# Merged distance-and-maximum operation in two attentions, and two more expert weight slots

## The chip, the cores and the metric

The kernel runs on 1 core of one Trainium2 chip. The metric is the device time of one execution in microseconds (us), the median of several runs. All data are float32. The engines that matter here are TensorE (PE, with its weight loads as PEld), VectorE (DVE), ScalarE (ACT), and SyncE (SP), whose queue issues nearly all DMA transfers.

## What is computed

Two transformer blocks over 256 tokens of width 1024. The first block has two layers; each has a mixer of three attentions (MLA, differential, sliding window), a cross-attention and a dense feed-forward. The second block is one layer with a recurrence, a pooling branch, a grouped attention, and a mixture of 16 experts. The change touches the scores of two of the attentions and the loading of the expert weights.

```python
# differential attention: 4 heads, 2 maps each
s = einsum('bqhmd,bshmd->bmhqs', qi, k2) * scale
s = s - slopes * abs(pos_q - pos_k)
p = softmax(s); a = p[:, 0] - lam * p[:, 1]
# sliding window: 8 heads, a sink per head
s = einsum('bnqkgd,bnskd->bnkgqs', qg, kb) * scale
s = s - slopes * dist; s = where(mask, s, lowest)
m = maximum(max(s), sink); e = exp(s - m)
p = e / (sum(e) + exp(sink - m))
...
# experts (expert choice): 16 experts, 32 tokens each, width 1024
# every expert's gate, up and down matrices are read once
```

## The kernel before

**Weights.** All weight matrices lie in one HBM array, `in_stream`, cut into units of 128 x 2048 float32 (1 MB). SP's queue copies them into SBUF slots in the order in which TensorE uses them. In the two layers there are 8 slots (5 called `ring`, 3 in `arena`), 64 units to a layer (L3417). In the second block the 35 dense units go through the 5 ring slots (`dense_unit`, L3426): unit v is issued when TensorE has finished the unit that held its slot, five units earlier. Each slot has a semaphore that counts its landings.

**Experts.** The last 192 units are the expert weights. They have 21 slots (`EXPERT_SLOTS`), made of the five ring slots and of pieces of `arena`, `par` and `const` that come free as the second block's other work ends. SP issues the first 14 (`EARLY_SLOTS`) as these pieces come free: three after the recurrence (`recurrence_left`), then in five batches (`BRANCHES_LEFT`), with the last dense units between them; then five ring slots as the dense units leave them, then two more. From the 22nd unit on, each waits until TensorE has used the unit that is 21 places before it (`expert_slots_used`, L3457). TensorE starts on the experts when the router has chosen the tokens.

**Attention scores.** Each layer works through 20 items in the order of `HEAD_ITEMS`: 4 MLA heads, 8 differential maps, 8 sliding-window heads. TensorE writes the scores of an item for both blocks of 128 tokens into one PSUM bank (L1034); differential and sliding-window items come in pairs and two banks (`both_tiles`) serve in turn, so that a pair waits until the banks of the pair before are read. VectorE then makes, for each differential or sliding-window item, one 128 x 512 operation that adds the distance times minus slope over scale to the raw scores (L1052), a maximum over each row (L1056), for a sliding-window head one more small operation with the sink (L1060), and the negated maximum (L1062, L1064). ScalarE takes the exponentials with the scale as an argument (L1077); VectorE normalises (L1094 to L1100) and for a second differential map subtracts (L1109); TensorE transposes (L1129); ScalarE copies the transposed tile (L1259) and TensorE multiplies by the values (L1162, L1178), whose result ScalarE copies out (L1250, L1255, L1888). All engines run their queues in program order. Between these steps TensorE runs fill work: three matmuls of the cross-attention's memory projections at each step (`MEMORY_HEADS`). After the last item VectorE forms differences of weights for the output projection (L740).

**Queries and keys.** Five units project them into columns; ScalarE copies each result from PSUM to `qk` (L1874), two 256-column pieces in one 128 x 512 operation: differential queries (j = 0), their keys (1), sliding-window queries (2, 3), their keys (4, 256 columns). Right behind j = 3 the memory rows are transposed (L203, L472) into the same two ScalarE banks (`act_tiles`) and copied with their gain (L490).

Of the kernel before, what the change touches and what calls it, by code (L numbers as in the profile page):

```python
# [20 lines left out]
S = 256  # L21
# [11 lines left out]
EARLY_SLOTS = 14  # L33
EXPERT_SLOTS = TOP_SLOTS + RING_SLOTS + 3
# [11 lines left out]
FAR = 1e30  # L46
LAYER_UNITS = 64
# [8 lines left out]
def columns(*parts):  # L56
# [9 lines left out]
    ("ident", 128), ("inv", 16), ("iota", 32), ("fold", E_N), ("eps", 1), ("ln_eps", 1), ("half_pi", 1),  # L66
# [20 lines left out]
GATE_UNITS = 12  # L87
ROUTER_ROWS = (0, 0, 0, E_N)
# [87 lines left out]
class Weights:  # L176
# [6 lines left out]
    def start(self, base, slots, loaded, free):  # L183

        self.n, self.base = 0, base
# [31 lines left out]
class Program:  # L217
    def __init__(self, nc, ctx, io):
# [8 lines left out]
                   *(f"expert_slot_loaded_{s}" for s in range(EXPERT_SLOTS)),  # L227
# [4 lines left out]
        self.expert_slot_loaded = [self.sem(f"expert_slot_loaded_{s}") for s in range(EXPERT_SLOTS)]  # L232
# [20 lines left out]
        self.expert_slots = (top[7:10] + ends + [top[0], top[1], top[5], top[12], halves, top[11]] + [top[4], top[6], top[10]]  # L253
# [681 lines left out]
SCALE = {"gqa": 64 ** -0.5, "diff": 32 ** -0.5, "swa": 64 ** -0.5, "mla": 96 ** -0.5, "x": 256 ** -0.5}  # L935
# [103 lines left out]
def softmax_max_dve(p, dve, i, item):  # L1039
# [15 lines left out]
    dve.e.wait_ge(p.both_tiles.drained, p.both_tiles.taken["dve"])  # L1055
    dve.e.tensor_reduce(mx, sc, AX, ALU.max).then_inc(dve.step(), 1)  # L1056
    dve.e.wait_ge(dve.steps, dve.n)
    if kind == "swa":
# [3 lines left out]
        dve.e.tensor_scalar(nm, mx, -1.0, None, ALU.mult).then_inc(dve.event("max_found"), 1)  # L1062
    else:
# [788 lines left out]
def layer_act(p, act, l, layer_par, mem_rows):  # L1852
# [17 lines left out]
    for j in range(5):  # L1870
# [3 lines left out]
        act.e.activation(p.qk[:, 2 * j:2 * j + n, :], shaped(bank[:, 0:n * S], n, S), ACT.Copy).then_inc(p.act_tiles.drained, 1)  # L1874
# [384 lines left out]
def second_pe(p, pe, w):  # L2259
    w.start(16 * DEPTH * LAYER_UNITS // SLOTS, p.ring_slots, p.slot_loaded, p.slots_free)  # L2260
# [1414 lines left out]
```

## Time and profile before

| | us |
|---|---|
| median of 3 runs | 1803.08 (1802.34 to 1803.63) |
| the profiled execution | 1804.25 |
| its span in the trace | 1802.5 |
| TensorE busy | 1627.3 (90%) |
| VectorE busy | 784.2 (44%) |
| ScalarE busy | 373.5 (21%) |
| HBM read | 383.65 MB |

The first layer runs to about 475 us, the second to about 935 us, the second block without its experts to about 1358 us, and the experts from there to the end. The page divides the span into 40 slices of 45 us: in the slices up to the 29th TensorE is at 9 tenths or more, and from the 32nd on the DMA engines are at 9 while TensorE falls to 6 or 7. A row of the timeline gives start, duration, engine, line, operation, output and inputs, count, and in square brackets how long the engine was idle before it and what released it.

### The profile page before, as it was taken

How to read it: one execution, taken by the hardware profiler on the slowest of the kernel's cores; microseconds unless marked ns; L12 is line 12 of the kernel's file. 1: busy time of each engine (PE TensorE's matmuls, PEld its weight loads, DVE VectorE, ACT ScalarE, POOL GpSimd, SP SyncE). 2: the span in 40 equal slices, each digit the busy share in tenths (PEclk: the TensorE clock that was granted, in tenths of full speed). 3: DMA queues.
4: the chain of work that ended last, by engine and by line, in shares of the span. 5: the costliest groups of instructions: out<-in, count | busy, mean ns of one | idle time of the engine just before them, and what ended most of it. 6: DMA issues, size and time to landing. Idle time of an engine off the chain costs nothing.

```text
span 1802.5 us, 26083 instructions
## 1 busy us (share of the span) xinstructions
PE 1627.3 (90%) x10862; PEld 1098.7 (61%) x10862; DVE 784.2 (44%) x1514; ACT 373.5 (21%) x953; POOL 2.2 (0%) x6
## 2 busy tenths in 40 slices
PE   8999999999999999999999999999999667667666
PEld 5867878884587787888558778888854101102011
DVE  3596567655539755765655583131421000000001
ACT  4253131110415412211021651111221000000001
POOL 0000000000000000000000000000000000000000
PEclk9999999999999999999999999999999866877766
DMA  9324335435542242543444231111788999999997
GB/s 388 118 71 145 136 118 203 182 146 188 219 145 75 105 167 77 197 187 146 187 164 147 87 116 51 49 59 63 303 323 325 421 421 421 421 421 420 421 420 321
DMA packets 55664, 386.35 MB, mean 214 GB/s; under 512 B 6272, under 2 KB 6784, under 8 KB 10752
## 3 DMA queue, kind: packets, MB, share of 16 engines
q1 hardware_dynamic: 53568, 375.15, 52.8%
q10 hardware_dynamic: 1984, 9.57, 1.4%
q8 instruction: 87, 1.43, 0.3%
q14 instruction: 25, 0.20, 0.0%
HBM read 383.65 MB, written 1.05 MB: 213 GB/s over the span
## 4 chain that ended last, share of the span: by engine, by line
PE 68%; DMA 22%; DVE 6%; ACT 2%; issue 1%; SPq 0%; PEldq 0%; DVEq 0%; PEld 0%; ACTq 0%
PE ps L199 49%; DMA arena<-in_stream 13%; DMA ring<-in_stream 6%; PE ps L2216 3%; DMA const<-in_stream 3%; PE ps L2197 3%; PE ps L1513 2%; PE ps L1034 2%; DVE small L1056 1%; PE ps L203 1%; DVE arena L1052 1%; PE ps L688 1%; PE ps L2357 1%; DVE arena L1100 1%; PE ps L1188 1%
## 5 line engine op out<-in xcount | busy, mean ns | idle before, releaser
L199 PE MATMUL ps<-arena 128*128 128x256 f32 (+4 forms) x2476 | 572.2, 498 | 77.3 <-DMA arena<-in_stream 71.9
L199 PEld LDWEIGHTS ps<-arena 128*128 128x128 f32 (+1 forms) x2476 | 324.2, 169 | 283.0 <-DMA arena<-in_stream 162.1
L199 PE MATMUL ps<-ring,arena 128*128 128x256 f32 (+5 forms) x1186 | 336.6, 526 | 39.3 <-DMA ring<-in_stream 34.4
L199 PE MATMUL ps<-arena,ring 128*128 128x256 f32 (+1 forms) x1228 | 284.2, 378 | 0.0
L199 PEld LDWEIGHTS ps<-ring,arena 128*128 128x128 f32 (+1 forms) x1186 | 177.6, 174 | 172.4 <-issue 76.4
L199 PEld LDWEIGHTS ps<-arena,ring 128*128 128x128 f32 x1228 | 221.1, 191 | 37.2 <-issue 9.9
L2527 PE MATMUL ps<-arena 128*32 128x512 f32 x230 | 153.7, 772 | 0.0
L2734 DVE TENSOR_TENSOR arena<-arena,ps 128x512 f32<-128x512 f32 x8 | 5.5, 687 | 250.5 <-PE ps L2527 250.5
L2749 DVE TENSOR_TENSOR x<-x,ps 128x512 f32<-128x512 f32 (+1 forms) x18 | 11.3, 628 | 139.3 <-PE ps L2629 139.3
L1077 ACT ACTIVATE arena<-arena,small 128x256 f32<-128x256 f32 x112 | 55.7, 498 | 76.0 <-DVE small L1064 76.0
L2527 PE MATMUL ps<-ring,arena 128*32 128x512 f32 x84 | 60.0, 816 | 0.0
L1660 ACT ACTIVATE arena<-arena 128x512 f32<-128x512 f32 x20 | 12.6, 630 | 179.4 <-DVE arena L1716 179.4
L1034 PE MATMUL ps<-arena 64*128 64x256 f32 (+3 forms) x256 | 46.8, 392 | 1.9 <-DVE arena L1052 1.3
L1690 DVE TENSOR_TENSOR arena<-ring,arena 128x1024 f32<-128x1024 f32 x38 | 45.4, 1221 | 2.1
L1056 DVE TENSOR_REDUCE small<-arena 128x2 f32<-128x512 f32 x56 | 38.4, 686 | 1.9
L1034 PEld LDWEIGHTS ps<-arena 64*128 64x128 f32 (+3 forms) x256 | 32.6, 187 | 10.0 <-issue 4.1
L1513 PE MATMUL ps<-arena 128*128 128x256 f32 x128 | 38.1, 379 | 0.0
L2216 PEld LDWEIGHTS ps<-arena 64*64 64x64 f32 x1152 | 34.4, 135 | 3.3 <-issue 3.3
L199 PE MATMUL ps<-par,arena 128*32 128x512 f32 x90 | 26.7, 823 | 10.0 <-DMA const<-in_stream 5.8
L2216 PE MATMUL ps<-arena 64*64 64x32 f32 x1152 | 35.5, 219 | 0.0
L1100 DVE TENSOR_SCALAR arena<-arena,small 128x256 f32<-128x256 f32 x112 | 34.5, 350 | 2.0
L1129 PE MATMUL ps<-const,arena 128*128 128x128 f32 x192 | 29.9, 279 | 4.6 <-ACT arena L1255 4.1
(431 smaller groups left out, 1887.1 us busy)
## 6 DMA issues: line engine op xcount, KB each, us to landing
arena<-in_stream SPq DMA_DIRECT2D x168, 1024.0 KB, 24.9
ring<-in_stream SPq DMA_DIRECT2D x160, 1024.0 KB, 6.4
par<-in_stream SPq DMA_DIRECT2D x9, 1024.0 KB, 26.7
const<-in_stream SPq DMA_DIRECT2D x9, 1024.0 KB, 27.0
par<-in_layer_par ACTq DMA_DIRECT2D x3, 1664.0 KB, 8.2
par<-in_stream SPq DMA_DIRECT2D x9, 512.0 KB, 24.2
const<-in_stream SPq DMA_DIRECT2D x9, 512.0 KB, 24.6
arena<-in_mem ACTq DMA_DIRECT2D x2, 1024.0 KB, 10.7
```

Of the source, the lines that this page charges most:

```text
L199: ins = self.pe.e.matmul(out, lhsT, rhs, start=start, stop=stop)
L203: return self._tell(self.pe.e.transpose(out, in_, identity))
L1034: ins = pe.e.matmul(bank[:, b * S:(b + 1) * S], a, k, start=j == 0, stop=j == len(parts) - 1)
L1056: dve.e.tensor_reduce(mx, sc, AX, ALU.max).then_inc(dve.step(), 1)
L1077: ins = act.e.activation(p.pr[i % 4][:, b, :], p.sc[i % 4][:, b, :], ACT.Exp, bias=nm[:, b:b + 1], scale=SCALE[kind], accum_out=sums[:, b: ...
L1100: ins = dve.e.tensor_scalar(pr[:, b, :], pr[:, b, :], sums[:, b:b + 1], None, ALU.mult)
L1129: ins = pe.e.transpose(bank[:, o:o + P], src[:, b, kb * P:(kb + 1) * P], p.c("ident"))
L1513: ins = (pe.e.matmul if end and last else w.mm)(out, left[:, k, :], right[:, k, :], start=k == 0, stop=end)
L1690: dve.e.tensor_tensor(t[n], a, b, ALU.subtract).then_inc(dve.event("weight_sums"), 1)
L2197: ins = pe.e.matmul(bank[r, o, :], a, b, start=j == 0, stop=j == len(ts) - 1)
L2216: ins = pe.e.matmul(bank[r, o, :].rearrange("p (g s) -> p g s", s=1 << n), left[r, o, :], rhs)
L2527: ins = (pe.e.matmul if e == GE - 1 else w.mm)(bank[r, :], src[:, k, r], slot_columns(u, e * 512, 512), start=k == 0, stop=k == KC - 1)
```

## The change

Three things are changed.

1. In differential and sliding-window items, the distance operation and the row maximum become one operation for each token block of 128 rows (`tensor_tensor_reduce` on 128 x 256): (scores minus distance) times slope, with the running maximum started from a very low number, or from the head's sink. The scale and the slope's inverse are moved into the query rows, so that the exponential's scale becomes 1.0.
2. For that, ScalarE's copies of the query projections (j = 0, 2, 3) are each made in two 128 x 256 operations with a factor for each row (`query_gain`, six new columns of the constants).
3. The SBUF that the compiler sets aside for DMA descriptors is cut to 512 bytes a partition, and two more expert slots (`spare`, 16 KB a partition) take its place. They are the first two of the slots' order, 23 in all, and are filled in the second block behind dense units 18 and 20. Their landings are counted on the semaphores of two layer slots, so the waits get a base for each slot.

```diff
-EARLY_SLOTS = 14
-EXPERT_SLOTS = TOP_SLOTS + RING_SLOTS + 3
+EARLY_SLOTS = 16
+SPARE_SLOTS = 2
+EXPERT_SLOTS = SPARE_SLOTS + TOP_SLOTS + RING_SLOTS + 3
...
+SPARE_AFTER = (18, 20)
...
-        self.pe.e.wait_ge(self.loaded[s], self.base + 16 * len(slot_parts(self.slots[s])) * (r + 1))
+        self.pe.e.wait_ge(self.loaded[s], self.bases[s] + 16 * len(slot_parts(self.slots[s])) * (r + 1))
...
+        spare = self.sb("spare", SPARE_SLOTS * UNIT)
+        spares = [spare[:, j * UNIT:(j + 1) * UNIT] for j in range(SPARE_SLOTS)]
+        self.expert_slots = (spares + top[7:10] + ends + [top[0], top[1], top[5], top[12], halves, top[11]] + [top[4], top[6], top[10]]
...
-SCALE = {"gqa": 64 ** -0.5, "diff": 32 ** -0.5, "swa": 64 ** -0.5, "mla": 96 ** -0.5, "x": 256 ** -0.5}
+DIFF_SCALE, SWA_SCALE = 32 ** -0.5, 64 ** -0.5
+SCALE = {"gqa": 64 ** -0.5, "diff": 1.0, "swa": 1.0, "mla": 96 ** -0.5, "x": 256 ** -0.5}
...
-        dve.e.scalar_tensor_tensor(sc, dist, -slope / scale, bank, ALU.mult, ALU.add).then_inc(p.both_tiles.drained, 1)
+        lowest = LOWEST if kind == "diff" else p.lp("sinks")[:, h:h + 1]
+        for b in range(NB):
+            ins = dve.e.tensor_tensor_reduce(sc[:, b, :], bank[:, b, :], dist[:, b, :], slope, lowest, ALU.subtract, ALU.max,
+                                             accum_out=mx[:, b:b + 1])
+            if b == NB - 1:
+                ins.then_inc(p.both_tiles.drained, 1)
+            else:
+                ins.then_inc(dve.step(), 1)
+        dve.e.wait_ge(dve.steps, dve.n)
+        dve.e.wait_ge(p.both_tiles.drained, p.both_tiles.taken["dve"])
+        dve.e.tensor_scalar(nm, mx, -1.0, None, ALU.mult).then_inc(dve.event("max_found"), 1)
...
-        dve.e.tensor_scalar(mx, mx, scale, p.lp("sinks")[:, h:h + 1], ALU.mult, ALU.max).then_inc(dve.step(), 1)
...
-        act.e.activation(p.qk[:, 2 * j:2 * j + n, :], shaped(bank[:, 0:n * S], n, S), ACT.Copy).then_inc(p.act_tiles.drained, 1)
+        if j in (1, 4):
+            act.e.activation(p.qk[:, 2 * j:2 * j + n, :], shaped(bank[:, 0:n * S], n, S), ACT.Copy).then_inc(p.act_tiles.drained, 1)
+        else:
+            for c in range(n):
+                at = (2 * j if j == 0 else 2 * j - 2) + c
+                ins = act.e.activation(p.qk[:, 2 * j + c, :], bank[:, c * S:(c + 1) * S], ACT.Copy,
+                                       scale=p.c("query_gain")[:, at:at + 1])
...
             for v in range(BLOCK2_UNITS - RING_SLOTS):
                 dense_unit(v)
+                if v in SPARE_AFTER:
+                    expert_unit(SPARE_AFTER.index(v))
             e.wait_ge(p.sem("recurrence_left"), 1)
-            for s in range(3):
+            for s in range(SPARE_SLOTS, SPARE_SLOTS + 3):
...
-    nc = bacc.Bacc("TRN2", target_bir_lowering=False, num_devices=1)
+    nc = bacc.Bacc("TRN2", target_bir_lowering=False, num_devices=1, dynamic_dma_scratch_size=512)
```

On VectorE in layer 0, the maximum of a second differential map and the normalising of the first map behind it, before (`arena` holds scores, distances and probabilities, `ps` is PSUM, `small` the row statistics):

```order
L1052 SCALAR_TENSOR_TENSOR arena<-arena,ps 128x512
L1056 TENSOR_REDUCE small<-arena 128x2
L1064 TENSOR_SCALAR small<-small 128x2
L1094 RECIPROCAL small<-small 128x2
L1100 TENSOR_SCALAR arena<-arena,small 128x256 x2
```

The same place in the changed kernel (ISA stands for the merged operation and for the row that reads its maximum out):

```order
L1066 ISA arena,small<-ps,arena 128x256
L1066 ISA small 128x1
L1066 ISA arena,small<-ps,arena 128x256
L1066 ISA small 128x1
L1074 TENSOR_SCALAR small<-small 128x2
L1110 RECIPROCAL small<-small 128x2
L1116 TENSOR_SCALAR arena<-arena,small 128x256 x2
```

Two rows of 512 columns became two of 256 columns with a one-column row behind each. Nothing else moves on VectorE there, except that a sliding-window item has one small row less.

On SP's queue, the second block's loads, before:

```order
L3426 DMA ring<-in_stream 128x2048 x30
L3434 DMA arena<-in_stream 128x2048 x3
L3426 DMA ring<-in_stream 128x2048
L3434 DMA par<-in_stream 128x2048
L3434 DMA const<-in_stream 128x2048
```

And in the changed kernel:

```order
L3452 DMA ring<-in_stream 128x2048 x19
L3460 DMA spare<-in_stream 128x2048
L3452 DMA ring<-in_stream 128x2048 x2
L3460 DMA spare<-in_stream 128x2048
L3452 DMA ring<-in_stream 128x2048 x9
L3460 DMA arena<-in_stream 128x2048 x3
L3452 DMA ring<-in_stream 128x2048
L3460 DMA par<-in_stream 128x2048
L3460 DMA const<-in_stream 128x2048
```

The first two expert units now stand among the dense units instead of behind the recurrence, and every later early load carries a unit that is two further on in the stream.

## Rows read from the trace of the kernel before

**Rows 1.** The page: busy tenths of PE, and GB/s, in 40 slices.
```profile
PE   8999999999999999999999999999999667667666
...
GB/s 388 118 71 145 136 118 203 182 146 188 219 145 75 105 167 77 197 187 146 187 164 147 87 116 51 49 59 63 303 323 325 421 421 421 421 421 420 421 420 321
```

**Rows 2.** Windows: stretch, length, busy us and (instructions) by engine, PEclk, DMA share, GB/s.
```profile
1350.00:1360.00 10.00, 9.15 (x56) 8.06 (x54) 5.91 (x18) 1.70 (x3) 0.00 (x0) 0.71 0.23 97
...
1400.00:1780.00 380.00, 256.06 (x1350) 47.97 (x1346) 19.91 (x37) 16.86 (x34) 0.00 (x0) 0.74 1.01 421
```

**Rows 3.** Chain that ended last, its last long piece: start, us, what.
```profile
1764.29 27.52 DMA arena<-in_stream
```

**Rows 4.** Timeline of PE at the last expert units.
```profile
1786.94 0.85 PE L199 MATMUL ps<-arena 128*32 128x256 f32 x11 [1.20 <-DMA arena<-in_stream]
...
1791.86 1.50 PE L199 MATMUL ps<-arena 128*32 128x256 f32 x11 [0.52 <-DMA arena<-in_stream]
```

**Rows 5.** Timeline of SP: dense units of the second block.
```profile
934.14 317.48 SPq L3426 DMA_DIRECT2D ring<-in_stream  x26
```

**Rows 6.** Timeline of PE, layer 0, attention: groups that it waited for.
```profile
107.33 1.14 PE L1034 MATMUL ps<-arena 64*128 64x256 f32 x8 [0.63 <-DVE arena L1052]
...
112.44 0.66 PE L1129 MATMUL ps<-const,arena 128*128 128x128 f32 x4 [0.22 <-DVE arena L1109]
...
116.02 1.10 PE L1178 MATMUL ps<-arena 128*128 128x64 f32 x8 [0.26 <-ACT arena L1259]
...
125.91 0.63 PE L1129 MATMUL ps<-const,arena 128*128 128x128 f32 x4 [1.15 <-ACT arena L1255]
...
134.12 1.08 PE L1162 MATMUL ps<-arena 128*64 128x256 f32 x8 [0.83 <-ACT arena L1259]
```

**Rows 7.** Windows over the attention of layer 0 and of layer 1.
```profile
84.49:136.93 52.44, 49.29 (x297) 36.24 (x297) 47.91 (x134) 30.48 (x101) 0.00 (x0) 1.00 0.18 61
546.60:599.00 52.40, 49.26 (x297) 36.20 (x298) 47.92 (x133) 30.40 (x101) 0.00 (x0) 1.00 0.18 61
```

**Rows 8.** Timeline of DVE: a differential item, then a sliding-window item.
```profile
85.65 0.69 DVE L1052 SCALAR_TENSOR_TENSOR arena<-arena,ps 128x512 f32<-128x512 f32 x1 [0.46 <-PE ps L1034]
86.38 0.69 DVE L1056 TENSOR_REDUCE small<-arena 128x2 f32<-128x512 f32 x1
87.10 0.17 DVE L1064 TENSOR_SCALAR small<-small 128x2 f32<-128x2 f32 x1
...
115.01 0.68 DVE L1052 SCALAR_TENSOR_TENSOR arena<-arena,ps 128x512 f32<-128x512 f32 x1
...
116.44 0.23 DVE L1060 TENSOR_SCALAR small<-small,par 128x2 f32<-128x2 f32 x1
116.70 0.17 DVE L1062 TENSOR_SCALAR small<-small 128x2 f32<-128x2 f32 x1
```

**Rows 9.** Timeline of DVE: two operations in a row from PSUM, 256 columns each.
```profile
149.88 0.74 DVE L802 TENSOR_TENSOR arena<-arena,ps 128x256 f32<-128x256 f32 x2
```

**Rows 10.** Groups by form: a 256-column DVE operation from PSUM: count, busy, mean ns.
```profile
L1714 DVE TENSOR_TENSOR arena<-arena,ps 128x256 f32<-128x256 f32 x20 | 8.4, 421 | 0.7
```

**Rows 11.** Timeline of ACT: exponentials with their accumulator reads.
```profile
87.30 0.51 ACT L1077 ACTIVATE arena<-arena,small 128x256 f32<-128x256 f32 x1 [1.21 <-DVE small L1064]
87.71 0.19 ACT L1077 ACTIVATION_READ_ACCUMULATOR arena<-arena,small 128x1 f32 x1
87.81 0.49 ACT L1077 ACTIVATE arena<-arena,small 128x256 f32<-128x256 f32 x1
```

**Rows 12.** Timeline of ACT and PE around the copy of query columns j = 3.
```profile
69.83 0.60 ACT L1874 ACTIVATE arena<-ps 128x512 f32<-128x512 f32 x1 [8.06 <-PE ps L519]
...
70.33 1.69 ACT L490 ACTIVATE arena<-ps,par 128x256 f32<-128x256 f32 x4
...
70.50 0.53 PE L203 MATMUL ps<-const,arena 128*128 128x128 f32 x3
```

**Rows 13.** The page: the DMA queue that carries the stream.
```profile
q1 hardware_dynamic: 53568, 375.15, 52.8%
```

More of the change, by code:

```diff
@@ L46 @@
 FAR = 1e30
+LOWEST = -3.0e38
 LAYER_UNITS = 64
@@ L181, in __init__, with start @@
         self.owed = 0
-    def start(self, base, slots, loaded, free):
-        self.n, self.base = 0, base
+    def start(self, bases, slots, loaded, free):
+        self.n, self.bases = 0, bases
         self.slots, self.loaded, self.free = slots, loaded, free
@@ L226, in __init__ @@
                    *(f"slot_loaded_{s}" for s in range(SLOTS)),
-                   *(f"expert_slot_loaded_{s}" for s in range(EXPERT_SLOTS)),
+                   *(f"expert_slot_loaded_{s}" for s in range(EXPERT_SLOTS - SPARE_SLOTS - RING_SLOTS)),
                    *(f"{ring}_tile_{what}" for ring in ("act", "dve", "both", "gate") for what in ("full", "drained")))
@@ L231, in __init__ @@
         ring = self.sb("ring", RING_SLOTS * UNIT)
-        self.expert_slot_loaded = [self.sem(f"expert_slot_loaded_{s}") for s in range(EXPERT_SLOTS)]
+        own = [self.sem(f"expert_slot_loaded_{s}") for s in range(EXPERT_SLOTS - SPARE_SLOTS - RING_SLOTS)]
+        rest = EARLY_SLOTS - SPARE_SLOTS
+        self.expert_slot_loaded = (self.slot_loaded[RING_SLOTS:RING_SLOTS + SPARE_SLOTS] + own[:rest]
+                                   + self.slot_loaded[:RING_SLOTS] + own[rest:])
+        layers, second = DEPTH * 16 * LAYER_UNITS // SLOTS, 16 * BLOCK2_UNITS // RING_SLOTS
+        self.expert_slot_base = ([layers] * SPARE_SLOTS + [0] * rest + [layers + second] * RING_SLOTS
+                                 + [0] * (len(own) - rest))
         self.expert_slots_used = self.sem("expert_slots_used")
@@ L251, in __init__ @@
         ends = [self.par[:, par_w - UNIT:par_w], self.const[:, CONST_W - UNIT:CONST_W]]
-        self.expert_slots = (top[7:10] + ends + [top[0], top[1], top[5], top[12], halves, top[11]] + [top[4], top[6], top[10]]
+        spare = self.sb("spare", SPARE_SLOTS * UNIT)
+        spares = [spare[:, j * UNIT:(j + 1) * UNIT] for j in range(SPARE_SLOTS)]
+        self.expert_slots = (spares + top[7:10] + ends + [top[0], top[1], top[5], top[12], halves, top[11]] + [top[4], top[6], top[10]]
                              + self.ring_slots + top[2:4])
@@ L1873, in layer_act @@
         n = 2 if j < 4 else 1
-        act.e.activation(p.qk[:, 2 * j:2 * j + n, :], shaped(bank[:, 0:n * S], n, S), ACT.Copy).then_inc(p.act_tiles.drained, 1)
+        if j in (1, 4):
[5 more added lines that the diff above has]
+                                       scale=p.c("query_gain")[:, at:at + 1])
+                if c == n - 1:
+                    ins.then_inc(p.act_tiles.drained, 1)
+                else:
+                    ins.then_inc(act.step(), 1)
         if j == 3:
@@ L2259, in second_pe @@
 def second_pe(p, pe, w):
-    w.start(16 * DEPTH * LAYER_UNITS // SLOTS, p.ring_slots, p.slot_loaded, p.slots_free)
+    w.start([16 * DEPTH * LAYER_UNITS // SLOTS] * RING_SLOTS, p.ring_slots, p.slot_loaded, p.slots_free)
     ready = token_rows(p, DEPTH)
@@ L2505, in second_pe @@
     w.flush()
-    w.start(0, p.expert_slots, p.expert_slot_loaded, p.expert_slots_used)
+    w.start(p.expert_slot_base, p.expert_slots, p.expert_slot_loaded, p.expert_slots_used)
     pe.e.wait_ge(p.sem("expert_rows"), 1)
@@ L3356, in _ @@
                 p.stage = f"layer_{l}"
-                w.start(l * (16 * LAYER_UNITS // SLOTS), p.slots, p.slot_loaded, p.slots_free)
+                w.start([l * (16 * LAYER_UNITS // SLOTS)] * SLOTS, p.slots, p.slot_loaded, p.slots_free)
                 layer_pe(p, pe, w, l)
@@ L3551, in constants @@
         c["fold"][32 * g + ROUTER_ROWS[g] + np.arange(E_N), np.arange(E_N)] = 1.0
+    half = t // 64
+    c["query_gain"] = np.stack([DIFF_SCALE / np.array(SLOPES)[8 + 2 * j + half] for j in range(2)]
+                               + [SWA_SCALE / np.array(SLOPES)[j + 4 * half] for j in range(4)], 1)
     c["eps"], c["ln_eps"], c["half_pi"] = [EPS], [LN_EPS], [math.pi / 2]
```

12 lines of the change are left out of this document (4 added, 8 removed).

## Prediction

> **What bounds the kernel now.** I read the page's slices first. TensorE is at 9 tenths from the second slice to the 31st, then at 6 or 7, while the transfers go to 421 GB/s in the 32nd slice and stay there [rows 1]. So there are two regimes: up to the experts TensorE's own queue sets the pace, and in the experts the weight stream does. The windows confirm the second: from 1400 to 1780 us the DMA engines are at a share of 1.01 and move 421 GB/s, and TensorE is busy 256.06 us of 380 [rows 2]. The chain of waits then ends in a transfer that was issued at 1764.29 us and landed at 1791.8 us [rows 3], and TensorE starts on that last unit at 1791.86 us [rows 4]. The span is 1802.5 us, so 10.7 us lie behind the last landing.
>
> Ahead of the experts the stream is no bound. In the slices 25 to 28 (1080 to 1260 us) it moves 49 to 63 GB/s [rows 1], and between 1350 and 1360 us it rests (share 0.23), since all 21 slots are full and TensorE has not begun to free them [rows 2]. A place that is filled earlier can therefore shorten the end.
>
> In the attention of a layer I read TensorE's waits. In layer 0 there are five over 0.1 us, each ended by VectorE or by a ScalarE operation: 0.63 + 0.22 + 0.26 + 1.15 + 0.83 = 3.09 us [rows 6]. The windows show the same in both layers: TensorE is busy 49.29 of 52.44 us and 49.26 of 52.40 us, so 3.15 and 3.14 us are idle, while VectorE is busy 47.91 and 47.92 us [rows 7]. VectorE is nearly full there, and its order (maximum of one item, normalising of the one before) delays the ScalarE queue, whose in-order copies TensorE then waits for.
>
> **The two slots.** One unit is 1.0486 MB, which at 421 GB/s is 2.49 us. From the moment at which TensorE frees its first slot, behind the pause at 1350 to 1360 us [rows 2], 192 - 21 = 171 units are still to be sent; afterwards 192 - 23 = 169. All run at the full rate, so the end comes 2 x 2.49 = 4.98 us earlier, wherever the start falls. What hides the two loads: the dense units of that part are issued 26 in 317.48 us, 12.2 us apart [rows 5], and a unit takes 2.49 us. A spare load behind one of them pushes no dense unit that TensorE is near to, since each is issued four units ahead of its use. Without that cover each would cost up to 2.49 us of TensorE's time, which would eat the gain. The early loads behind the recurrence are the same number as before (14 and 5 and 2), at the same events, and their cover is the pause at 1350 us. The bases on the semaphores change no wait's end. Sum: -5.0 us.
>
> **The merged operation.** Before, a differential item holds VectorE from 85.65 us to the start of the negation at 87.10 us, 1.45 us; a sliding-window item from 115.01 to 116.70 us, 1.69 us [rows 8]. No row of before shows the merged operation, so I bound it. Low: it costs as a 256-column operation that reads PSUM, 0.42 us alone [rows 10], while two in a row take 0.74 us, so the second starts 0.32 us after the first [rows 9]. For the read of the maximum I take ScalarE's accumulator read: 0.19 us long, and it moves the next operation by 0.10 us (87.71 to 87.81) [rows 11]. An item is then 0.32 + 0.10 + 0.32 + 0.19 + 0.03 for the wait = 0.96 us, and 1.08 us for a sliding-window head, whose start value is read from memory (0.23 against 0.17 us for such a small operation, so 0.06 for each block [rows 8]). VectorE gains 0.49 us on 8 items and 0.61 us on 8, that is 8.8 us in a layer. High: the merged operation walks its 256 columns in the time of 512, 0.69 us [rows 8], and nothing overlaps: 2 x (0.69 + 0.19) + 0.03 = 1.79 us, a loss of 0.34 and 0.22 us, 4.5 us in a layer. I take the low end, since the L1052 row already reads PSUM and SBUF together, multiplies and adds, and costs per column what the maximum alone costs (0.69 and 0.69 us); a running maximum is one more step on the same column.
>
> A rule speaks against this edit. The Trainium skill, "VectorE: DVE Perf Modes", section "The DRAIN you can't avoid", says that the next operation does not start until the pipe is empty, and the errata section before it that small tiles pay a fixed latency each. By it the item would be 2 x 0.42 + 2 x 0.19 + 0.03 = 1.25 us instead of 0.96, still below 1.45. The 0.74 us of the row of two stands against the strict form [rows 9].
>
> What TensorE gets of VectorE's 8.8 us is only its own idle time; behind that it is the bound itself. With each maximum half a microsecond or more earlier, the exponentials, ScalarE's copies and the transposes are ready before TensorE asks. The worst one, 1.15 us at 125.91 us, comes behind the item at which VectorE also makes the squares for the differential norm (L1956, L1958) and a memory copy (L990), some 2 us by the price of 0.69 us for such a row; a lead of 0.6 us an item over the items before it covers the wait. One wait stays in part: the pair of scores at 107.33 us needs both banks read, and the merged form frees a bank after 0.32 + 0.10 + 0.42 = 0.84 us instead of 0.68; I keep 0.15 us of the 0.63. Each wait that goes also gives back the overlap of neighbouring groups, about 0.1 us, 0.45 us in all. So -3.09 + 0.15 - 0.45 = -3.4 us a layer, -6.8 us in both. What is late next is TensorE's own queue, and behind this stretch it has work until the experts, so the gain moves the start of the experts.
>
> **The split copies.** ScalarE has been idle for 8.06 us before the copy of j = 3 [rows 12], and the copies of j = 0 and 2 stand alone behind 30 matmuls each, so only j = 3 matters. Its copy at 69.83 us takes 0.60 us, and TensorE's third group of transposes starts at 70.50 us in the bank that it frees at 70.43 us [rows 12]. Two 256-column copies with a factor take half of the 1.69 us that four take [rows 12], 0.85 us, so TensorE starts 0.2 to 0.3 us later: +0.25 us a layer, +0.5 us. The bounds are 0 and 0.5 us a layer.
>
> **The sum.** 1804.25 (the profiled execution) - 5.0 - 6.8 + 0.5 = 1792.95 us. It lies 1.17 us above the median of the runs, so on the median the forecast is 1803.08 - 11.3 = 1791.8 us. About 1.75 us lie around the span and don't change.
>
> **Rivals.**
> A. VectorE's gain is real, but TensorE's waits come back elsewhere (the latency from scores to transposed tile, not VectorE's load, sets them). For it: four of the five waits name operations that stand behind others in order. Against it: VectorE's 47.9 of 52.4 us. It leaves 1803.08 - 5.0 + 0.5 = 1798.6 us. Chance 0.12.
> B. The slots give nothing: the end is set by TensorE's half clock and not by the stream. TensorE's granted clock is 0.74 on average in this stretch, between its levels of 1.2 and 2.4 GHz, and the same group takes 0.85 us or 1.50 us [rows 2, 4]. Against it: DMA share 1.01 throughout, and TensorE waited 1.20 and 0.52 us for data ahead of these two groups at either clock. It gives 1803.08 - 6.3 = 1796.8 us. Chance 0.04.
> C. The merged operation runs at the high price, and VectorE becomes the bound of the attention. Its load grows by 4.5 us against 4.5 us of idle time in a 52.4 us stretch; if TensorE waits for none to all of it, that is 0 to 9.0 us in both layers: 1798.6 to 1807.6 us, middle 1803. This is the case on the slow side. It turns the sign of the whole from 4.1 us more TensorE waiting a layer (3.6 + 5.0 - 0.5 = 8.1 us in both), 0.25 us on each of the 16 items. Chance 0.07: 0.02 faster, 0.02 within the bound, 0.03 slower. The Trainium skill, "Vector Engine (DVE) Microarchitecture Reference", section "Points that are easy to get wrong", says that an accumulating operation on two non-bf16 SBUF sources halves its throughput; here one source is PSUM, and no row of before shows such an operation.
> D. The cut of the descriptor space slows the stream. For a slower kernel the 427 us of streaming would have to lengthen by 15 us, 421 down to 407 GB/s. Against it: the bytes go over a queue of the kind hardware_dynamic [rows 13]. Time from 1792 to 1808 us; chance 0.03, 0.01 for each sign. The Trainium skill, "DMA: Bandwidth & Descriptors", section "SWDGE vs HWDGE vs iDMA", says that only transfers issued by GpSimd keep descriptor rings in SBUF; by it D falls away.
>
> **How the numbers follow.** The forecast has 0.74. Its own range: better by the 0.3 us left at the scores, the 0.5 us of the copies, 0.9 us if the overlap is worth 0.2 us instead of 0.1 us a wait, and about 1.9 us if TensorE's clock is at its upper level behind the last landing (0.85 for 1.50 us [rows 4], and the matmuls behind it in proportion), 1788 us; worse by half of the attention's gain, 1795 us. Range with the rivals A and B: 1788 to 1799 us. 0.2% is 3.6 us, about what a measurement of this kernel can tell from no change. Faster by more than that: 0.74 + 0.12 + 0.04 + 0.02 + 0.01 = 0.93; within it 0.02 + 0.01 = 0.03; slower 0.03 + 0.01 = 0.04.
>
> **What would show it.** In the profile after: the merged row at 0.42 us and the read under 0.2 us, VectorE about 39 us busy in the stretch that had 47.9, and TensorE's idle time there under 0.7 us. The same first scores in layer 1 about 3.2 us earlier, the experts' first unit about 6.3 us earlier, the last landing 11.3 us earlier, DMA share 1.01 and 421 GB/s in between. A merged row near 0.7 us, or new waits of TensorE at the transposes, would prove the second term wrong; a pause of the stream after the first freed slot, or a TensorE wait for a ring unit near dense unit 19, the first.

## The result and the profile after

The changed kernel takes 1790.93 us (median of 4 runs, 1790.43 to 1792.95) against 1803.11 us of the kernel before beside it (4 runs, 1802.34 to 1803.63). The ratio is 0.9934, 95% interval 0.9919 to 0.995. A second set of 5 runs on another occasion gave 1791.03 us against 1802.93 us, ratio 0.9934 again, interval 0.9921 to 0.9948. So it is 12 us faster; the forecast was 1791.8 us. The profiled execution has a span of 1791.0 us.

The page's slices after (TensorE and GB/s, the answers to [rows 1]):

```profile
PE   8999999999999999999999999999999766666666
GB/s 390 119 72 165 117 134 189 188 149 190 212 152 84 118 143 93 193 177 170 187 144 163 73 142 73 49 50 73 280 322 333 421 420 420 421 421 421 421 421 320
```

The two regimes stand as before. The windows over the attention of the two layers and over the expert stage (span, then busy time of PE, PEld, DVE, ACT, POOL, granted clock, DMA share, GB/s), to be laid beside [rows 7] and [rows 2]:

```profile
84.50:132.80 48.30, 47.96 (x297) 36.59 (x297) 38.18 (x158) 31.42 (x101) 0.00 (x0) 1.00 0.19 66
542.78:591.00 48.22, 48.05 (x298) 36.65 (x297) 38.31 (x158) 31.26 (x102) 0.00 (x0) 1.00 0.19 66
1400.00:1770.00 370.00, 247.07 (x1322) 46.89 (x1326) 19.91 (x37) 17.15 (x35) 0.00 (x0) 0.75 1.01 421
```

The attention stretch is 4.1 us shorter in each layer, TensorE is idle in it for 0.34 and 0.17 us, and VectorE is busy 38 us where it was busy 47.9. The stream still runs at a share of 1.01 and 421 GB/s.

VectorE's timeline of one differential item and one sliding-window item, the answer to [rows 8]:

```profile
85.67 0.42 DVE L1066 CUSTOM_DVE_ANT_0 arena<-ps,arena 128x256 f32<-128x256 f32 x1 [0.46 <-PE ps L1046]
86.02 0.08 DVE L1066 DVE_READ_ACCUMULATOR2_ANT small<- 128x1 f32 x1
86.02 0.42 DVE L1066 CUSTOM_DVE_ANT_0 arena<-ps,arena 128x256 f32<-128x256 f32 x1
86.36 0.08 DVE L1066 DVE_READ_ACCUMULATOR2_ANT small<- 128x1 f32 x1
86.55 0.17 DVE L1074 TENSOR_SCALAR small<-small 128x2 f32<-128x2 f32 x1
...
113.02 0.48 DVE L1066 CUSTOM_DVE_ANT_0 arena<-ps,arena,par 128x256 f32<-128x256 f32 x1 [0.26 <-PE ps L1046]
113.43 0.08 DVE L1066 DVE_READ_ACCUMULATOR2_ANT small<- 128x1 f32 x1
...
114.02 0.17 DVE L1074 TENSOR_SCALAR small<-small 128x2 f32<-128x2 f32 x1
```

From the first operation to the negation it is 86.55 - 85.67 = 0.88 us for a differential item (1.45 before) and 114.02 - 113.02 = 1.00 us for a sliding-window one (1.69 before).

TensorE's first scores of the last head pairs of layer 0, from its timeline, with the one wait over 0.1 us that is left of the five in [rows 6]:

```profile
101.08 1.13 PE L1046 MATMUL ps<-arena 32*128 32x256 f32 x8
106.67 1.13 PE L1046 MATMUL ps<-arena 64*128 64x256 f32 x8 [0.34 <-DVE small L1066]
111.85 1.13 PE L1046 MATMUL ps<-arena 64*128 64x256 f32 x8
117.42 1.14 PE L1046 MATMUL ps<-arena 64*128 64x256 f32 x8
123.32 1.13 PE L1046 MATMUL ps<-arena 64*128 64x256 f32 x8
```

Before, the pairs that follow the first (84.49 us) stood at 90.38, 95.88, 101.21, 107.33, 113.14, 119.24 and 126.47 us; after, at 90.40, 95.90, 101.08, 106.67, 111.85, 117.42 and 123.32 us. The steps between pairs were 5.89, 5.50, 5.33, 6.12, 5.81, 6.10, 7.23 us and are 5.90, 5.50, 5.18, 5.59, 5.18, 5.57, 5.90 us. The gain is 0, 0, 0.15, 0.53, 0.63, 0.53 and 1.33 us, and the rest, 0.9 us, stands behind the last pair.

**Lining up the traces.** All these kernels issue the same 10862 matmuls in the same order, so the starts of equal matmuls can be compared, and a stretch is the time between two of them. In us: from the first differential scores to the second half of the last head pair's products (84.49 to 134.12 us before), for both layers; the stretch ahead of it with the query copies; from the first matmul to the first expert unit; and from the first load into a slot that TensorE has freed to the last landing, with the units in it.

| kernel | attention, layer 0 | layer 1 | copies, layer 0 | layer 1 | first expert unit | last stretch (units) |
|---|---|---|---|---|---|---|
| before | 49.63 | 49.64 | 24.59 | 16.58 | 1352.95 | 431.54 (171) |
| after | 45.57 | 45.41 | 24.83 | 16.82 | 1346.25 | 427.43 (169) |
| after, second profile | 45.56 | 45.41 | 24.83 | 16.82 | 1345.14 | 427.08 (169) |

The last stretch begins with the row of SyncE's timeline (after) and ends with the last step of the chain of waits (start, duration), which answers to [rows 3]; the tail behind it answers to [rows 4]:

```profile
1353.46 0.33 SPq L3460 DMA_DIRECT2D spare<-in_stream  x1
```

```profile
1728.87 24.73 DMA ring<-in_stream
1753.66 27.23 DMA arena<-in_stream
```

```profile
1780.93 1.33 PE L202 MATMUL ps<-arena 128*32 128x256 f32 x11 [0.54 <-DMA arena<-in_stream]
```

1753.66 + 27.23 = 1780.89 us is the last landing, 10.9 us earlier than before (1791.81), and 10.1 us of the span lie behind it (10.7 before).

### The profile page after: what moved, and what is told of

It reads as the page before. It is cut to its first block, busy times and chain, and to the rows that moved or that the text cites. A ratio compares the mean times of both kernels' runs of the same rounds, so it can differ in the third digit from the quotient of the medians.

```text
span 1791.0 us, 26168 instructions
## 1 busy us (share of the span) xinstructions
PE 1618.8 (90%) x10862; PEld 1098.8 (61%) x10862; DVE 764.7 (43%) x1562; ACT 376.5 (21%) x959; POOL 2.1 (0%) x6
## 4 chain that ended last, share of the span: by engine, by line
PE 73%; DMA 21%; DVE 2%; ACT 2%; issue 1%; SPq 0%; DVEq 0%; ACTq 0%
PE ps L202 52%; DMA arena<-in_stream 11%; DMA ring<-in_stream 10%; PE ps L2242 3%; PE ps L2223 3%; PE ps L1046 2%; PE ps L1529 2%; PE ps L206 1%; PE ps L1145 1%; PE ps L699 1%; PE ps L1178 1%; PE ps L2383 1%; PE ps L1204 1%; PE ps L1630 0%; PE ps L530 0%
## 5 line engine op out<-in xcount | busy, mean ns | idle before, releaser
L202 PE MATMUL ps<-arena 128*128 128x256 f32 (+4 forms) x2396 | 556.8, 491 | 69.3 <-DMA arena<-in_stream 63.8
L202 PE MATMUL ps<-ring,arena 128*128 128x256 f32 (+4 forms) x1132 | 324.8, 512 | 31.8 <-DMA ring<-in_stream 27.2
L2553 PE MATMUL ps<-arena 128*32 128x512 f32 x208 | 140.8, 781 | 0.0
L2760 DVE TENSOR_TENSOR arena<-arena,ps 128x512 f32<-128x512 f32 x8 | 5.5, 688 | 250.6 <-PE ps L2553 250.6
L2775 DVE TENSOR_TENSOR x<-x,ps 128x512 f32<-128x512 f32 (+1 forms) x18 | 11.3, 628 | 133.7 <-PE ps L2655 133.7
L2553 PE MATMUL ps<-ring,arena 128*32 128x512 f32 x80 | 51.5, 746 | 0.0
L1046 PE MATMUL ps<-arena 64*128 64x256 f32 (+3 forms) x256 | 46.8, 392 | 1.0 <-DVE small L1066 0.5
L1046 PEld LDWEIGHTS ps<-arena 64*128 64x128 f32 (+3 forms) x256 | 32.3, 187 | 9.2 <-issue 4.8
L202 PE MATMUL ps<-spare,arena 128*32 128x512 f32 (+1 forms) x124 | 23.8, 688 | 13.9 <-DMA spare<-in_stream 13.8
L202 PE MATMUL ps<-par,arena 128*32 128x512 f32 (+1 forms) x94 | 25.3, 772 | 10.7 <-DMA par<-in_stream 6.1
L1732 DVE TENSOR_TENSOR arena<-arena,ps 128x512 f32<-128x512 f32 x20 | 13.8, 688 | 44.8 <-PE ps L1529 44.8
```

Source lines behind the costliest of these rows:

```text
L202: ins = self.pe.e.matmul(out, lhsT, rhs, start=start, stop=stop)
L1046: ins = pe.e.matmul(bank[:, b * S:(b + 1) * S], a, k, start=j == 0, stop=j == len(parts) - 1)
L2553: ins = (pe.e.matmul if e == GE - 1 else w.mm)(bank[r, :], src[:, k, r], slot_columns(u, e * 512, 512), start=k == 0, stop=k == KC - 1)
```

## The experiments

Each kernel was timed in turn with the kernel before, whose medians in the three sets were 1802.9, 1803.3 and 1802.9 us. The theory at this point: each of VectorE's items sets when banks and probabilities come free, TensorE waited on that, and the merged form removes it; the slots are worth their bytes. Rivals: the gain of the attention is smaller and the rest is the clock or the slots; the gain of the slots is smaller because the early loads cost something.

**The attention part alone, and the slots alone.** `attn_only` is the changed kernel with SPARE_SLOTS back at 0 and the descriptor space of before:

```diff
-EARLY_SLOTS = 16
-SPARE_SLOTS = 2
+EARLY_SLOTS = 14
+SPARE_SLOTS = 0
...
-SPARE_AFTER = (18, 20)
+SPARE_AFTER = ()
...
```

> The changed kernel with its attention part alone (merged operation, slope in the query rows, split copies): the two spare slots, their two early loads and the cut descriptor space are gone. If the gain sits as the two traces show it (TensorE 8.05 us earlier behind the second layer's attention, 0 to 1 us lost behind it), the time is 1795 us (1794.6 to 1796). By the sum of the prediction (6.3 us net) it is 1796.8 us. By rival A (waits come back elsewhere) 1803 us. Second question: in the changed kernel TensorE's granted clock is at half level for 3.4 us around 1096 us, which costs 2.4 us there. If the spare loads caused it, it is not here, and the first expert unit starts 8 us or more ahead of the kernel before; if it comes by chance or from the earlier start of the second block, it may stand here too, and the first unit starts 6 to 7 us ahead.

`slots_only` is the changed kernel with the subtraction, the maximum and the copies of before.

> The kernel before with the two spare slots, their loads behind dense units 18 and 20 and the cut descriptor space; the attention is that of before. By the prediction's term 1803.1 - 5.0 = 1798.1 us; by the two traces (169 units took 427.4 us against 431.5 us for 171) 1803.1 - 4.1 = 1799.0 us. Rival B (the end hangs on TensorE's half clock) 1803.1 us, DMA share below 1.01. Rival D (the cut space slows the stream) fewer than 421 GB/s and 1803 us or more. If the spare loads cause the half-clock stretch of 3.4 us in the second block, this kernel has it behind dense unit 20 as well, and TensorE reaches the experts 2 us later than before, which makes 1800 to 1801 us.

Measured: the attention alone 1794.89 us, ratio 0.9954 (0.9941 to 0.9968), that is 8.0 us; the slots alone 1799.31 us, ratio 0.9982 (0.9973 to 0.9991), that is 3.6 us (1.6 to 4.9). Together 11.6 us of the 12: the two parts add up. The lined-up stretches:

| kernel | attention, layer 0 | layer 1 | copies, layer 0 | layer 1 | first expert unit | last stretch (units) |
|---|---|---|---|---|---|---|
| attn_only | 45.56 | 45.40 | 24.83 | 16.82 | 1344.98 | 431.61 (171) |
| slots_only | 49.63 | 49.63 | 24.59 | 16.58 | 1353.76 | 426.25 (169) |

Rival A (the waits come back) is refuted: it wanted 1803 us for the first. Rivals B and D are refuted by the second and by its window, which moves what before moved (no run cuts the descriptor space without adding the slots):

```profile
1400.00:1770.00 370.00, 245.38 (x1323) 44.67 (x1315) 17.14 (x33) 13.82 (x28) 0.00 (x0) 0.75 1.01 421
```

**The split copies alone.** The kernel before with this edit and factors of 1:

```diff
-        act.e.activation(p.qk[:, 2 * j:2 * j + n, :], shaped(bank[:, 0:n * S], n, S), ACT.Copy)...
+            for c in range(n):
+                ins = act.e.activation(p.qk[:, 2 * j + c, :], bank[:, c * S:(c + 1) * S], ACT.Copy,
+                                       scale=p.c("query_gain")[:, at:at + 1])
```

> The kernel before, with the query copies of j = 0, 2 and 3 split into two 256-column ScalarE copies each with a factor read from memory, all factors 1. By the prediction's term TensorE's third group of transposes starts 0.2 to 0.3 us later in each layer: 1803.6 us (bounds 1803.1 and 1804.1). By the two traces the group starts at 70.50 us in both kernels, so 1803.1 us. In the profile: the copies of j = 3 take 0.85 us together; the third group starts at 70.7 to 70.8 us by the prediction, at 70.5 us if something else sets it.

Measured: 1804.46 us, ratio 1.0008 (0.9999 to 1.0017), which alone says only that it is no gain. The lined-up traces decide: the stretch with the copies is 24.83 and 16.82 us instead of 24.59 and 16.58, so 0.24 us a layer. My expectation "0 by the two traces" was a misreading: the third group starts at 70.50 us in both kernels, but the groups ahead of it had come 0.22 us earlier in the profile after. TensorE's timeline after, the groups of transposes; the step to the third is 0.65 us, before it was 70.50 - 70.07 = 0.43 us:

```profile
69.41 0.49 PE L206 MATMUL ps<-const,arena 128*128 128x128 f32 x3
...
69.85 0.49 PE L206 MATMUL ps<-const,arena 128*128 128x128 f32 x3
...
70.50 0.55 PE L206 MATMUL ps<-const,arena 128*128 128x128 f32 x3
```

**The price of the merged item.** The changed kernel, with the first block's merged operation made once or twice more:

```diff
+            for again in range(1 if b == 0 else 0):
+                dve.e.tensor_tensor_reduce(sc[:, b, :], bank[:, b, :], dist[:, b, :], slope, lowest, ALU.subtract, ALU.max,
+                                           accum_out=mx[:, b:b + 1]).then_inc(dve.step(), 1)
+                dve.e.wait_ge(dve.steps, dve.n)
```

> The changed kernel with the merged operation of the first token block made twice, the second behind the first's end: 0.45 us more VectorE time on each of the 16 items, 7.2 us a layer (38.2 to 45.4 of a stretch of 48.3 us). This prices the merged item. If what counts is that VectorE's load stays below TensorE's time, and the queue catches up between items, little comes back: 1791 to 1793 us. If each item's own time counts, as before, 0.45 of the 0.57 us (differential) and 0.69 us (sliding window) that the change saves on an item come back, 71% of 8.05 us: 1796.6 us. Halfway, with waits only where VectorE has other work beside the items (the differential norm), 1793 to 1795 us.

> The changed kernel with the merged operation of the first block made three times: 0.90 us more on each item, 1.78 us for a differential one (the price of rival C) and 1.90 us for a sliding-window one, 14.4 us a layer. One more gave back 8 us of 8.2. If VectorE is the bound from there on, the second 0.45 us costs its full 7.2 us a layer: 1799.3 + 14.4 = 1813.7 us. By rival C's own working (idle time of TensorE from none to all) the time is at most 1807.6 us plus the 0.25 us an item that this goes beyond it. If half of it hides behind TensorE, 1806 us.

Measured: once more 1799.33 us, ratio 0.9982 (0.9973 to 0.9991); twice more 1814.14 us, ratio 1.0063 (1.0048 to 1.0078). The first was slower than each of its three expectations. A sliding-window item with one more, from VectorE's timeline:

```profile
113.24 0.48 DVE L1067 CUSTOM_DVE_ANT_0 arena<-ps,arena,par 128x256 f32<-128x256 f32 x1
...
113.77 0.48 DVE L1070 CUSTOM_DVE_ANT_0 arena<-ps,arena,par 128x256 f32<-128x256 f32 x1
...
114.77 0.17 DVE L1078 TENSOR_SCALAR small<-small 128x2 f32<-128x2 f32 x1
```

One more costs 0.47 us on a differential item and 113.77 - 113.24 = 0.53 us on a sliding-window one, 8.0 us a layer: the items are 1.35 and 1.53 us long with one more, and 1.82 and 2.06 us with two. Attention stretches: 49.22 and 49.57 us with one, 56.34 and 57.14 us with two. So the first 8.0 us costs TensorE 3.7 and 4.2 us a layer, and the second 7.1 and 7.6 us. With two more, half-clock stretches of 3.4 us stand in the attention, one in layer 0 and two in layer 1; the matmuls in each took 1.6 us longer. In layer 0 nearly all of that is made up: TensorE starts its last products there without a wait, while it waits 1.44 us for them in layer 1. Taken from whichever layer has no such stretch at that point, the attention is 56.3 us long, so the second 8.0 us costs 6.7 us, most of it. TensorE's waits in the attention of layer 0 (total, times, longest), with one more and with two:

```profile
PE ps L1046 <- DVE small L1070: 2.5, 4, 1.1
PE ps L1149 <- ACT arena L1275: 0.4, 1, 0.4
PE ps L1182 <- ACT arena L1279: 0.4, 1, 0.4
```

```profile
PE ps L1046 <- DVE small L1070: 6.3, 6, 1.7
```

The waits sit at the scores (L1046), for a bank that VectorE has not let go. The program text has the coupling: the merged form frees the bank with the item's last long operation, while the separate form freed it after the subtraction, half way. That fits one more, which with items of 1.35 and 1.53 us takes as long in the attention, to 0.4 us, as before with 1.45 and 1.69 us. It is a reading of where the waits stand; no run frees the bank earlier at an equal length of the item.

**Merging the sliding-window items only.** The differential items get the two operations of before again (and their query columns a factor of 1):

```diff
-    if kind in ("diff", "swa"):
+    if kind == "diff":
+        dve.e.scalar_tensor_tensor(sc, p.dist, -SLOPES[h + 8] / scale, bank, ALU.mult, ALU.add)...
+        dve.e.tensor_reduce(mx, sc, AX, ALU.max)...
+    elif kind == "swa":
```

> The changed kernel with the merged operation on the eight sliding-window items alone; the eight differential items have the scaled subtraction and the separate maximum of before again. The traces of before and after give per pair of scores, in layer 0, a gain of 0, 0, 0.15, 0.53, 0.63, 0.53 and 1.33 us and 0.9 us behind the last: nearly all of it stands at the sliding-window items. Theory one, each item's own time counts where it stands: this kernel keeps about 7.5 of the 8.2 us, 1791.5 us. Theory two, VectorE's order carries lateness on from item to item, so that a slow differential item makes the first sliding-window pairs late: the eight differential items give back their 0.57 us each in part, 1.5 to 3 us in both layers, 1792.5 to 1794 us.

Measured: 1794.93 us, ratio 0.995 (0.9937 to 0.9964). The median lies above both ranges, with runs from 1792.19 to 1795.93 us, so the traces have to decide. Attention 46.56 and 46.40 us, so 1.0 us a layer comes back, 2.0 us in all, inside theory two's 1.5 to 3 us and above theory one's 0.7 us. Compared matmul by matmul with the changed kernel, 0.6 us of it in each layer stands at sliding-window pairs, whose own items are unchanged: a pair's lateness is made in part by the items ahead. The rest stands at the differential pairs. The largest piece is the wait at the first sliding-window pair, 0.63 us as before where the changed kernel has 0.34 and 0.17 us, and it names VectorE's differential subtraction:

```profile
107.93 1.13 PE L1046 MATMUL ps<-arena 64*128 64x256 f32 x8 [0.63 <-DVE arena L1062]
```

**Where the spare loads stand.** First both behind dense unit 29, then both behind the recurrence, with no dense unit to hide behind (the edit is that of the second):

```diff
-SPARE_AFTER = (18, 20)
+SPARE_AFTER = ()
...
-            for s in range(SPARE_SLOTS, SPARE_SLOTS + 3):
+            for s in range(SPARE_SLOTS + 3):
```

> The changed kernel with both spare loads behind dense unit 29, the last one ahead of the recurrence, back to back, instead of behind 18 and 20. If their place is free, as the prediction has it, the time is 1791 us. The half-clock stretch of 3.4 us near 1096 us, which stood in the changed kernel's profile but neither in the kernel with the slots alone nor in the one without them: if it comes by chance it is not here, and the first expert unit starts 8 to 9 us ahead of the kernel before; if it hangs on a load at that place with the block's earlier start, it is gone too, and the median falls by 2 us to 1789 us; with chance it stays at 1791 us.

> The changed kernel with the two spare loads behind the recurrence, ahead of the three arena loads there, instead of behind dense units 18 and 20: their cover (12.2 us between dense units) is gone. The slots still count 23. Every load behind the recurrence comes 5 us later. If the pause of the stream ahead of the experts (before: 8 us, after: 5 to 6 us) takes it, the time stays at 791 over a thousand, 1791 us. If the dense ring units that TensorE waits for late in the block are pushed by 5 us and TensorE has no reserve there, up to 2 x 2.49 = 5 us come back: 1796 us, the price that the prediction gave for a lost cover.

Measured: 1790.79 us, ratio 0.993 (0.9917 to 0.9944), and 1790.05 us, ratio 0.9931 (0.9917 to 0.9944). Neither place costs anything, and TensorE waits for no load between 60 us and the experts in either ("791 over a thousand" in the second expectation is a slip for 1791). The first unit comes at 1343.52 and 1343.95 us after the first matmul, the last stretch is 426.35 and 427.32 us. Why the second is free shows in the transfers between 1260 and 1360 us (busy share in tenths in 40 slices of 2.5 us): they dip to 3 tenths near 1332 us and rest from 1345 us to 1351 us. In this part SyncE's queue waits for TensorE's matmuls (the longest wait is 14.7 us), so the last loads wait for slots to come free and not for the transfers.

```profile
DMA  0049999999999999999999999995734996002989
```

**The half-clock stretch near 1096 us.** In the profile after, and not in that of before, TensorE's granted clock was at its lower level, 1.2 GHz, for 3.4 us there. The window over it, after and in the second profile of the same kernel:

```profile
1095.00:1100.00 5.00, 4.57 (x38) 3.59 (x35) 1.46 (x5) 0.00 (x0) 0.00 (x0) 0.66 0.02 5
```

```profile
1095.00:1100.00 5.00, 5.00 (x96) 4.41 (x95) 1.12 (x4) 0.77 (x4) 0.00 (x0) 1.00 0.01 3
```

> The changed kernel once more, unedited, beside the next two. Time 1791 us (1790 to 1792). Its profile answers whether the half-clock stretch near 1096 us, which cost 2.3 us of TensorE there, belongs to the kernel: if it does it stands there again, and the first expert unit starts 6 to 7 us ahead of before; if it comes by chance, 7.7 us ahead or more (8.16 us of attention less 0.48 us of copies, give or take the stretches that before has near 1011 and 1349 us).

Measured: 1791.03 us, and the stretch is not there. None of the ten profiles of the other experiments has it either, though five of them have the loads at the same place. So it is chance, not the change; matmul by matmul it cost the first profile 2.0 us of TensorE beside the second one. What brings it up in one execution stays open.

**A further version.** The merged operation on the other softmax items too (subtracting a zero column), and then, with it, the copies of j = 3 whole again, their factors applied in place behind the memory columns, and the spare loads behind unit 29:

```diff
-        dve.e.tensor_copy(sc, bank)...
-        dve.e.tensor_reduce(mx, sc, AX, ALU.max)...
+        for b in range(NB):
+            ins = dve.e.tensor_tensor_reduce(sc[:, b, :], bank[:, b, :], p.c("zero").to_broadcast([P, S]), 1.0, LOWEST,
+                                             ALU.subtract, ALU.max, accum_out=mx[:, b:b + 1])
...
-        if j in (1, 4):
+        if j in (1, 3, 4):
...
+            for c in range(2):
+                act.e.activation(p.qk[:, 6 + c, :], p.qk[:, 6 + c, :], ACT.Copy,
+                                 scale=p.c("query_gain")[:, 4 + c:5 + c]).then_inc(act.step(), 1)
```

> The changed kernel with the merged operation on the other 24 softmax items too (subtracting a zero column): 1.37 us of copy and maximum become 0.77 us on each. None of TensorE's waits in the changed kernel's profile over 0.1 us names these items' VectorE operations except one of 0.5 us in the second block; the others name ScalarE's copies. If only named waits count, 1790.5 us. If VectorE's shorter items also bring ScalarE's copies forward (waits of 0.9, 0.7 and 0.6 us in each layer), up to 4 us less, 1787 us.

> The kernel with the merged operation on all 40 softmax items of a layer pair and the second block, both spare loads behind dense unit 29, and the copies of j = 3 made in one operation again, with the two factors applied in place in SBUF behind the memory columns. In each layer the third group of transposes should start as in before: the 0.24 us a layer of the split copies go, 0.5 us in all. With the 1.1 us that the merged operation on the other items brought in the trace (0.57 us a layer): 1789.5 us, against 1791 us of the changed kernel. If the in-place factors hold ScalarE's queue where TensorE waits, no gain: 1790 us or more.

Measured: 1790.03 us, ratio 0.9923 (0.9909 to 0.9936), and 1789.25 us, ratio 0.9924 (0.9911 to 0.9938), the second beside 1791.03 us of the changed kernel. The intervals of these ratios overlap that of the changed kernel, so the times alone don't rank them. The lined-up traces do: with the first, the stretch between the two layers' attentions is 395.1 us instead of 395.7, as much is saved behind layer 1, and the attention of layer 0 is 45.40 us instead of 45.56: 1.3 us in all. With the second, the copy stretches are back at 24.59 and 16.58 us, and 0.3 us more is saved behind layer 1: 2.1 us in all ahead of the second block, beside 1.8 us between the medians.

## Why the prediction was right, point by point

**The bound.** Confirmed. Both regimes are where [rows 1, 2] had them, and the two parts of the change act each in its own regime and add up (8.0 and 3.6 us).

**The slots, -4.98 us.** The mechanism holds. By the times it is 3.6 us (1.6 to 4.9), its upper end just short of the term. By the traces the last stretch takes 431.54, 431.61 and 431.59 us in the three profiles with 171 units, and 426.25 to 427.43 us, 426.73 us on average, in the ten with 169: 4.85 us less. The first profile of the changed kernel is the longest of the ten, so it alone would have shown only 4.1 us; the scatter of 1.2 us between executions is why one pair of profiles does not size this term.

The cover was misjudged. The prediction hid the two loads behind the dense units and said that each would cost up to 2.49 us without them. The run with both behind the recurrence has no such cover and costs nothing. The spare time of the queue ahead of the experts is larger than the one pause that the prediction named.

**The merged operation's own price.** Predicted 0.96 and 1.08 us an item, measured 0.88 and 1.00. The operation takes 0.42 us and the next starts 0.34 to 0.35 us after it, close to the 0.32 us of [rows 9]. What was too high is the read of the maximum: ScalarE's, 0.19 us long and worth 0.10 us to the next operation [rows 11], stood in for it; VectorE's is 0.08 us, and the next merged operation starts in the same instant (86.02 us for both). Another error cancels a part of this: the negation starts 86.55 - 86.44 = 0.11 us after the last read ends, where the prediction had 0.03 us for the wait. The start value from memory costs 0.06 us a block, as taken. VectorE's busy time fell by 9.7 us in layer 0 and 9.6 us in layer 1, predicted 8.8. The strict reading of the Trainium skill, "VectorE: DVE Perf Modes", section "The DRAIN you can't avoid", made an item 1.25 us; but the same section adds that a next operation that is not held starts earlier. The trace shows the second: 0.42 us operations start 0.35 us apart. Where a semaphore wait stands between them, as in the run with one more, they start 0.47 us apart.

**TensorE's share of it, -3.4 us a layer.** Direction and mechanism right, size too small: 49.63 - 45.57 = 4.06 and 49.64 - 45.41 = 4.23 us, 8.3 us in both, where 6.8 stood. Compared matmul by matmul, the 4.06 us of layer 0 have three parts. The idle time at the five waits fell by 2.74 us (2.90 in layer 1), where 3.09 - 0.15 = 2.94 was predicted. The overlap of neighbouring groups at these waits gave 0.72 us in both layers, where the prediction had 0.45. The last 0.60 us (0.62 in layer 1) stands at places where TensorE had no wait over 0.1 us: steps between matmuls at the scores, the transposes and the products that were 0.03 to 0.12 us longer before. This third part the prediction put at nothing, since it read only the waits over 0.1 us; it is the larger half of what is missing. The overlap and most of these delays are not idle time: by the windows in layer 0 (52.44 us before, 48.30 after) TensorE's idle time fell by 2.8 us and its busy time by 1.33 us, with the same matmuls, because a matmul behind such a delay is shown longer (0.32 us against 0.27 us at the transposes). The steps between pairs of scores hold both: the pair from 119.24 to 126.47 us took 7.23 us against 5.90 us now, 1.33 us, for 1.15 us of named wait.

Of the waits, the one that was to stay did stay, at the place and for the reason given (two banks to be read): 0.34 us in layer 0 and 0.17 us in layer 1, predicted 0.15.

**The split copies, +0.25 us a layer.** Measured 0.24 us in both layers, in each kernel that has them, and gone in the one that has the j = 3 copy whole.

**The sum.** -8.3 + 0.5 - 4.9 = -12.7 us by the lined-up traces; -12.2 us by the medians; the forecast was -11.3. Of its three terms two were right to 0.15 us, and the attention's was 1.5 us too small.

**The sights.** First scores of layer 1 about 3.2 us earlier: 3.9 us, counted from the first scores of layer 0, in both profiles of the changed kernel. First expert unit 6.3 us earlier: 6.7 us with the half-clock stretch at 1096 us in it, 7.8 us in the second profile without, although that one came to layer 0's attention 1.3 us later. Last landing 11.3 us earlier: 10.9 us. VectorE about 39 us busy: 38.2. TensorE idle less than 0.7 us: 0.34.

**Rival C**, the slow side, did not come, since its condition (0.69 + 0.19 us a block) did not. But its price was wrong. The run with two more has items of 1.82 and 2.06 us, 5.9 us more VectorE work a layer than before. The rival's working capped TensorE's loss at VectorE's own growth, 4.5 us a layer, and would cap it here at 5.9. The run shows 56.34 - 49.63 = 6.7 us in layer 0, and 7.5 us in layer 1 with the half-clock stretches that were not made up. The step that failed there is to start from the kernel before: the merged form holds the bank longer, and it breaks even near items of 1.35 and 1.53 us and not at 1.45 and 1.69. By the times that case gave 1814 us, above the 1807.6 us named as its end; up to 2.9 us of that is the run's VectorE work beyond the rival's price.

## What to carry to other kernels

When a nearly full engine hands buffers to the one that sets the pace, read the steps between equal groups on the waiting engine (here from one pair of scores to the next), not only its named waits: the named waits gave 2.7 of the 4.1 us. When two operations become one, ask which buffer the first of them used to free and when; here the merged one frees it at its end, and breaks even at a shorter item than the one it replaced. And two profiles of equal instruction order can be subtracted matmul by matmul: that separates 0.24 us that 11 timed runs left at 0 to 3 us, as long as the starting points are lined up first.

## What the runs showed of the hardware

- A VectorE operation that reads PSUM and SBUF (128x256, f32), subtracts, multiplies and keeps a running maximum takes 0.42 us, as long as a plain one that reads PSUM [rows 10], and 0.48 us with its start value from memory. The read of its maximum is a row of 0.08 us that the next operation does not wait for: the starts are 0.35 us apart, and 0.47 us with a semaphore wait in between.
- TensorE's granted clock falls to its lower level for 3.4 or 6.8 us at a few places ahead of the experts, and in which of them differs between executions of one kernel. The stretch near 1004 us stands in the first profile of the changed kernel (3.4 us) and not in the second; the one near 1341 to 1345 us was 3.4 us there and 6.8 us in the second. Beside the second profile, those near 1004 and 1096 us cost the first 1.7 and 2.0 us, and the shorter one near 1345 us gave back 1.2 us. The first expert unit, counted from the first matmul, lies only 1.1 us apart, because the second profile had lost 1.3 us right at the start: equal matmuls stood 0.69 us apart there until about 16.5 us, and 0.35 us apart from about 13.8 us on in the first. The factor of two looks like the lower level too, but no record of the granted clock covers that part.
- The descriptor space cut to 512 bytes, with every transfer of the weight stream issued by SyncE, left the stream at 421 GB/s.
